# A finished attention pair leaves the accumulator bank later in the slot: ScalarE's part behind exponentials and copies, VectorE's part one slot on

## The chip, the cores and the metric

The kernel runs on one core of a Trainium2 chip. The metric is the device time of one execution, in microseconds. A core has TensorE (PE, matmuls and transposes into eight accumulator banks called PSUM), ScalarE (ACT: exponentials, copies), VectorE (DVE: reductions, multiplications, subtractions), GpSimd (POOL) and SyncE (SP), which here only load data. Each runs its own list of instructions; they meet by semaphores.

## What is computed

Two transformer blocks of two layers each, one after the other, on 512 tokens of width 1024, in float32. Precision is kept by splitting: every operand x of the large products is held as a high part and a low part x - high, and a product is three matmul passes. The parts that matter here are four attention stages. Cut to their core:

```python
# stage "fox" (first block, layer 2): 2 pairs of memory heads (256 keys), then 6 pairs of causal heads
logits = q @ k.T * scale + cum_logf[q] - cum_logf[k]; p = softmax(causal(logits)); o = p @ v
# stage "sparse" (second block, layer 1): 4 pairs of heads over chosen keys
p = softmax(where(chosen, q @ k.T * scale, -inf)); o = p @ v
# stage "dif" (second block, layer 2): 8 heads of two softmaxes each
a = softmax(q0 @ k0.T) - lam * softmax(q1 @ k1.T); o = a @ v
o = rms_norm(o, subln_g) * (1 - lambda_init)          # per head, then the output projection
```

The first memory attention (first block, layer 1) is a fourth stage of the same kind, which accumulates in one bank.

## The kernel before

The attention stages are one class, `Mixed` (line 1393). A stage has pairs of heads (in dif, a pair is one head with its two softmaxes). A pair is cut into four units, one for each 128 queries; unit `qt` of a causal pair sees `(qt+1)*128` keys. The stage runs in slots, numbered from 0. In slot s the three engines do, each in the order given:

- TensorE (`tensor`): the logits of unit s (L1481, L1487), half of the slot's share of projection matmuls, called fill (L430), the transposes of the probabilities of unit s-1 (`turn`, L1495), the product with the values of unit s-2 (`value`, L1519), the rest of the fill. The logits of unit s go into a pair of banks that unit s-2 used, so they wait for ScalarE's copy of the transposed probabilities of unit s-2 (signal `turned_act`).
- ScalarE (`scalar`): the exponentials of unit s (L1589, two instructions and their row sums), each waiting for VectorE's maximum; the copy of the transposed probabilities of unit s-1 (L1570); then, for a projection tile that has come in, in dif four part copies for the rotation (L698, only in even slots), and the high part of a weight strip (L369 or L373).
- VectorE (`vector`): the maxima of unit s (L1637 or L1640), the taking of projection tiles (L626, or in dif L705, L707, L709, which wait for L698), the low part of a weight strip (L396 or L401), the scaling of the probabilities of unit s (`scale`, L1616 to L1624), which waits for the exponentials.

In the sparse stage and from unit 24 of fox on (`t >= self.deep`) a third set of banks is used, the transposes lie one slot later, the copies of ScalarE stand ahead of the exponentials, and the scaling of unit s-1 stands ahead in VectorE's slot s.

The output of a pair (128 x 512) gathers in one bank. `self.outs` names it for each pair; in fox, sparse and dif two banks take turns. When a pair's fourth unit is done, `take_scalar` and `take_vector` empty the bank, in the slot that `taken_at` gives: slot 4n+6 for pair n, one later in the deep part. In fox and sparse ScalarE copies the bank out as the high part (L1672) and VectorE subtracts it from the bank for the low part (L1680). In dif ScalarE copies it to `difQ` (L1746) and squares that into `difK` (L1748); VectorE has nothing in `take_vector`. There the class `HeadNorm` goes on: in slot 26, at its end, TensorE sums the squares of heads 0 to 5 (`mean`, L1091), waiting for each; later slots take the root, spread it (L1098), scale each head (L1776), and form its high (L1756) and low part (L1781). In slots 26 to 31 some matmuls without a use (L1104) keep TensorE's clock up.

Before the change both takes stand early in their slot: ScalarE's is its first instruction, ahead of the copies and exponentials; VectorE's stands after the maxima and ahead of projection tiles and weight strips. A value product of pair n+2 waits for the emptying of pair n, four slots on.

Of the kernel before, what the change touches and what calls it, by code (L numbers as in the profile page):

```python
# [19 lines left out]
QT = SEQ // P  # L20
# [35 lines left out]
def build(nc, a, out):  # L56
    ctx = ExitStack()
    with ctx:
# [168 lines left out]
        class Signal:  # L227
# [3 lines left out]
            def __init__(self, name, engine):  # L231
                self.sem = ctx.enter_context(nc.semaphore(name))
                self.count = START
                self.engine = engine
                Signal.made.append(self)
# [60 lines left out]
        class NoErrands:  # L296
# [4 lines left out]
            def scalar(self, act, st):  # L301
                pass
# [1090 lines left out]
        class Mixed(Stage):  # L1393
# [6 lines left out]
            def __init__(self, pairs, sets, fill=(), pace=None, values_ready=None, apart=False, source=(hH, hL), norm=None, beside=None, probs=tmpB, turns=probsT,  # L1400
                         busy=(), busy_bank=0, deep=None, deep_sets=None, outs=None, first_use=(), last_split=None, late=None):
                super().__init__()
                self.busy, self.busy_bank = dict(busy), busy_bank
                self.pairs, self.sets, self.fill, self.apart, self.source = pairs, sets, fill, apart, source
                self.values_ready, self.norm, self.beside, self.probs, self.turns = values_ready, norm, beside, probs, turns
                self.units = [(n, pair, qt) for n, pair in enumerate(pairs) for qt in range(QT)]
                n = len(self.units)
                self.deep, self.outs, self.first_use = n if deep is None else deep, outs or [OUT_BANK] * len(pairs), dict(first_use)
                self.banks = [(sets if t < self.deep else deep_sets)[t % len(sets if t < self.deep else deep_sets)] for t in range(n)]
                self.buffers = list(sets) + [b for b in deep_sets or () if b not in sets]  # L1410
                lags = [1 if t >= self.deep else 0 for t in range(n)]
                self.slots = n + 3 + lags[-1]
                self.scaled_at, self.turned_at, self.valued_at, self.taken_at = [[[t for t in range(n) if t + later + lags[t] == s]
                                                                                  for s in range(self.slots + 2)] for later in (0, 1, 2, 3)]
                self.logits0, self.max0, self.exp0 = logits_in.reserve(2 * n), max_in.reserve(2 * n), exp_in.reserve(2 * n)
                self.scaled0, self.turned0, self.tact0 = scaled.reserve(n), turned_in.reserve(2 * n), turned_act.reserve(2 * n)
                self.value0 = value_in.reserve(n)
                self.gate = PairGate(pairs) if norm is None else norm.attach(pairs)
                self.taken0 = heads_taken.reserve(len(pairs)) if norm else 0
                self.before = [(bank_read[b], bank_read[b].count) for first in sets for b in (first, first + 1) if b < RING]  # L1420
                self.last_split, self.last_fill = last_split, fill[-1].strips[-1].tiles[-1] if fill else None
                self.late = late
                self.plan(pace)

            def plan(self, pace):
# [147 lines left out]
            def scalar(self, act):  # L1573
                units = len(self.units)
                for s in range(self.slots + 1):
                    for t in self.taken_at[s]:
                        if self.units[t][2] == QT - 1:
                            self.take_scalar(act, self.units[t][0])
                    for t in self.turned_at[s]:
                        if t >= self.deep:  # L1580
                            self.copy_turned(act, t)
                    if s < units:
                        n, pair, qt = self.units[s]
                        seen, bank = self.seen(s), self.bank(s)
                        for hh in range(2):
                            c = self.mine(s) + hh
                            act.wait_ge(max_in.sem, self.max0 + 2 * s + hh + 1)
                            to = self.prob(s, hh)[:, 0:seen]
                            act.activation(to, ps[:, bank + hh, 0:seen] if pair.row is None else to, ACT.Exp, bias=neg_max[:, c:c + 1],  # L1589
                                           scale=1.0 if pair.row is None else -1.0, accum_out=row_sum[:, c:c + 1]).then_inc(exp_in.sem, 1)  # L1590
                    for t in self.turned_at[s]:
                        if t < self.deep:
                            self.copy_turned(act, t)
                    for tile in self.copies[s]:
                        tile.strip.run.take.scalar_tile(act, tile)
                        if tile is tile.strip.tiles[-1] and (tile is not self.last_fill or self.last_split is None):
                            split_high(act, tile.strip.n + 2)
                    if self.last_split and s == self.last_split[0]:
                        split_high(act, self.last_fill.strip.n + 2)
                    if self.norm:  # L1600
                        self.norm.scalar_slot(act, s)
                    if self.late:
                        self.late.scalar_slot(act, s)
                    if self.beside:
                        self.beside.scalar_slot(act, s)
                if self.beside:
                    self.beside.scalar_rest(act)
# [18 lines left out]
            def vector(self, dve):  # L1626
                units = len(self.units)
                for s in range(self.slots + 1):
                    if s < units:
                        n, pair, qt = self.units[s]  # L1630
# [11 lines left out]
                    for t in self.scaled_at[s]:  # L1642
                        if t >= self.deep:
                            self.scale(dve, t)
                    for t in self.taken_at[s]:
                        if self.units[t][2] == QT - 1:
                            self.take_vector(dve, self.units[t][0])
                    if self.beside:
                        self.beside.vector_between(dve, s)
                    for tile in self.takes[s]:  # L1650
# [6 lines left out]
                    for t in self.scaled_at[s]:  # L1657
                        if t < self.deep:
                            self.scale(dve, t)
                    if self.norm:  # L1660
                        self.norm.vector_slot(dve, s)
                    if self.late:
# [1338 lines left out]
        for name, v in vectors:  # L3001
            r0, n = row_of[name], v.shape[0]
            while n:
# [3 lines left out]
                r0, n = r0 + m, n - m  # L3007
# [119 lines left out]
```

## Time and profile before

| | us |
|---|---|
| median of 3 runs | 2564.92 (2561.49 to 2565.49) |
| profiled execution, device time | 2560.56 |
| its span, first to last instruction | 2558.9 |
| TensorE busy | 2500.8 (98%) |
| VectorE busy | 1532.8 (60%) |
| ScalarE busy | 1053.4 (41%) |
| mean granted TensorE clock | 0.999 |

The span is what the trace shows; 1.7 us of the device time lie around it. A row of the timeline gives the start from the beginning of the span, the duration, the engine, the line of the kernel, the operation, output and inputs, and in brackets the idle time of the engine ahead of it with what ended it. Neighbouring equal instructions are merged (x4). A busy TensorE is not one at its peak, and ends of matmuls are modelled.

### The profile page before, as it was taken

The numbers are of one execution on the slowest core, as the hardware profiler recorded it, in microseconds if no ns is written. First come the engines' busy times: TensorE is split into PE (matmuls) and PEld (weight loads), VectorE is DVE, ScalarE is ACT, GpSimd is POOL, SyncE is SP. The second block draws the span as 40 slices with busy tenths as digits, with TensorE's granted clock in tenths as the row PEclk, the third lists the DMA queues.
The fourth block names the chain that finished last, engine by engine and source line by source line (L and its number), as shares of the span: only waits on it lengthen the run. The fifth ranks groups of instructions, "written<-read, shape, count | busy, mean of one in ns | idle before, by whom it ended". The sixth has DMA issues, their size and how long they took to land.

```text
span 2558.9 us, 31124 instructions
## 1 busy us (share of the span) xinstructions
PE 2500.8 (98%) x12413; PEld 1966.4 (77%) x12413; DVE 1532.8 (60%) x2299; ACT 1053.4 (41%) x1629; POOL 76.2 (3%) x154
## 2 busy tenths in 40 slices
PE   8999999999998999999999999999999989999999
PEld 6667877778866877777777578888878767888887
DVE  6996788686555487867667653333264775533334
ACT  5354433334555342323644743222254763522223
POOL 2000000000000001000000000000000000000000
PEclk9999999999999999999999999999999999999999
DMA  6123466553222256554321023323223112233321
GB/s 177 52 80 99 120 194 182 162 169 96 82 77 80 70 163 204 165 166 141 86 92 54 1 66 116 98 83 99 82 66 99 50 34 84 83 98 99 95 79 58
DMA packets 328095, 262.46 MB, mean 103 GB/s; under 512 B 13658, under 2 KB 312862, under 8 KB 327952
## 3 DMA queue, kind: packets, MB, share of 16 engines
q1 hardware_dynamic: 312256, 206.13, 27.2%
q0 software_dynamic: 15696, 54.34, 6.7%
q8 instruction: 99, 1.62, 0.3%
q14 instruction: 44, 0.36, 0.0%
HBM read 258.32 MB, written 2.12 MB: 102 GB/s over the span
## 4 chain that ended last, share of the span: by engine, by line
PE 88%; DVE 4%; ACT 4%; DVEq 1%; issue 1%; SPq 0%; DMA 0%; ACTq 0%; PEldq 0%; PEld 0%
PE ps L430 59%; PE ps L444 6%; PE ps L448 6%; PE ps L452 6%; PE ps L1481 2%; PE ps L2103 1%; PE ps L2631 1%; PE ps L1495 1%; PE ps L1519 1%; ACT tmpB L1589 1%; DVE wL L396 1%; ACT probsT L1570 1%; ACT wH L369 1%; ACT tmpA L698 1%; DVE tmpB L1640 0%
## 5 line engine op out<-in xcount | busy, mean ns | idle before, releaser
L396 DVE TENSOR_TENSOR wL<-raw,wH 128x2048 fp32r<-128x2048 f32 (+1 forms) x184 | 413.0, 2245 | 122.1 <-ACT wH L369 116.3
L369 ACT ACTIVATE wH<-raw 128x2048 fp32r<-128x2048 f32 (+1 forms) x184 | 343.7, 1869 | 237.1 <-PE ps L430 100.0
L430 PE MATMUL ps<-hH,wH 128*128 128x512 f32 x1656 | 427.7, 400 | 0.1
L430 PE MATMUL ps<-hH,wL 128*128 128x512 f32 x1656 | 425.2, 399 | 0.0
L430 PE MATMUL ps<-hL,wH 128*128 128x512 f32 x1656 | 424.8, 399 | 0.0
L430 PEld LDWEIGHTS ps<-hH,wH 128*128 128x128 f32 x1656 | 308.2, 188 | 84.7 <-issue 13.7
L430 PEld LDWEIGHTS ps<-hH,wL 128*128 128x128 f32 x1656 | 309.6, 188 | 82.4 <-issue 10.8
L430 PEld LDWEIGHTS ps<-hL,wH 128*128 128x128 f32 x1656 | 309.9, 188 | 76.4 <-issue 4.5
L1066 DVE TENSOR_TENSOR tmpB<-ps,tmpB 128x512 f32<-128x512 f32 x44 | 30.4, 691 | 228.2 <-PE ps L430 228.2
L1003 ACT ACTIVATE tmpA<-ff_up,cols 128x512 f32<-128x512 f32 x88 | 67.0, 809 | 237.9 <-DVEq L1030 237.9
L444 PE MATMUL ps<-gH,wH 128*128 128x512 f32 x480 | 154.6, 399 | 2.5 <-issue 1.0
L448 PE MATMUL ps<-gH,wL 128*128 128x512 f32 x480 | 153.1, 396 | 0.2 <-DVE wL L396 0.2
L452 PE MATMUL ps<-gL,wH 128*128 128x512 f32 x480 | 138.1, 396 | 0.0
L1040 DVE SCALAR_TENSOR_TENSOR tmpA<-ff_up,cols,tmpA 128x510 f32<-128x510 f32 (+1 forms) x176 | 124.3, 748 | 22.8 <-ACT tmpA L1003 17.1
L1964 DVE SCALAR_TENSOR_TENSOR mod_acc<-mod_ring,silu_c,mod_acc 128x1024 f32<-128x1024 f32 x84 | 107.7, 1282 | 45.6 <-DMA mod_ring<-w_mod 43.1
L1057 ACT ACTIVATE gH<-tmpB 128x512 fp32r<-128x512 f32 x44 | 27.8, 632 | 235.0 <-DVE tmpB L1066 235.0
L430 PE MATMUL ps<-gH,wH 128*128 128x512 f32 x480 | 122.8, 396 | 0.5 <-ACT mod L1993 0.5
L430 PE MATMUL ps<-gL,wH 128*128 128x512 f32 x480 | 122.4, 395 | 0.0
L430 PE MATMUL ps<-gH,wL 128*128 128x512 f32 x480 | 122.4, 395 | 0.0
L790 DVE SCALAR_TENSOR_TENSOR xT<-ps,mod_plus,xT 128x512 f32<-128x512 f32 x56 | 41.2, 748 | 133.8 <-PE ps L452 73.0
L444 PEld LDWEIGHTS ps<-gH,wH 128*128 128x128 f32 x480 | 90.2, 189 | 26.2 <-issue 2.9
L448 PEld LDWEIGHTS ps<-gH,wL 128*128 128x128 f32 x480 | 90.2, 188 | 22.3 <-DVE wL L396 1.0
(407 smaller groups left out, 3284.4 us busy)
## 6 DMA issues: line engine op xcount, KB each, us to landing
raw<-w_up SPq DMA_DIRECT2D x132, 512.0 KB, 5.3
mod_ring<-w_mod POOLq DMA_DIRECT2D x96, 512.0 KB, 4.3
raw<-w_down SPq DMA_DIRECT2D x32, 1024.0 KB, 5.9
raw<-w_gate SPq DMA_DIRECT2D x44, 512.0 KB, 4.0
raw<-w_down SPq DMA_DIRECT2D x16, 768.0 KB, 4.3
raw<-w_in_even SPq DMA_DIRECT2D x9, 1024.0 KB, 5.2
raw<-w_out SPq DMA_DIRECT2D x8, 1024.0 KB, 5.1
raw<-w_in_odd SPq DMA_DIRECT2D x16, 512.0 KB, 5.1
```

The source lines that it names most:

```text
L369: last = act.activation(wH[:, st.part, 0:st.size], raw[:, st.slot, 0:st.size], ACT.Copy)
L396: last = dve.tensor_tensor(wL[:, st.part, 0:st.size], raw[:, st.slot, 0:st.size], wH[:, st.part, 0:st.size].bitcast(F32), ALU.subtract)
L430: last = pe.matmul(dst, left, right, start=(t == 0 and k == 0), stop=(t == 2 and k == self.kt - 1))
L444: pe.matmul(dst, *operands(wH, srcH, k), start=(k == order[0]), stop=False)
L448: return pe.matmul(dst, *operands(wL, srcH, k), start=False, stop=False)
L452: return pe.matmul(dst, *operands(wH, srcL, k), start=False, stop=(k == order[-1]))
L790: dve.scalar_tensor_tensor(x, t, mod_plus[:, g:g + 1], x, ALU.mult, ALU.add).then_inc(bank_read[tile.bank].sem, 1)
L1003: last = act.activation(tmpA[:, 2 * u + f, :], ff_up[:, 2 * u + f, :], ACT.Identity, bias=self.bias(s, f), scale=self.weight(2, s, f))
L1040: dve.scalar_tensor_tensor(t, ff_up[:, 2 * u + f, 0:SEQ - back], self.weight(2 - back, s, f), t, ALU.mult, ALU.add)
L1066: dve.tensor_tensor(ff_tmp[:, s % 2, :], ps[:, value.bank, :], tmpB[:, s % 2, :], ALU.mult).then_inc(ff_prod.sem, 1)
L1481: mm = pe.matmul(ps[:, bank + hh, 0:seen], pair.q[lo:lo + DH, qt * P:qt * P + P], pair.k[lo:lo + DH, 0:seen], start=True, stop=True)
L1964: dve.scalar_tensor_tensor(mod_acc[:, :], mod_ring[:, u, :], silu_c[:, k:k + 1], mod_acc[:, :], ALU.mult, ALU.add).then_inc(mod_free[u], 1)
```

## The change

In stages whose output banks alternate (fox, sparse and dif; not the first memory attention), ScalarE's take moves from the head of the slot to behind the exponentials of unit s and the copy of unit s-1, still ahead of projection tiles and weight strips. VectorE's take moves to the end of the next slot's list, behind that slot's maxima, tiles, strips and scaling. No instruction is added or removed.

```diff
+                self.alternating = len(set(self.outs)) > 1
...
             def scalar(self, act):
                 for s in range(self.slots + 1):
-                    for t in self.taken_at[s]:
-                        if self.units[t][2] == QT - 1:
-                            self.take_scalar(act, self.units[t][0])
+                    done = [self.units[t][0] for t in self.taken_at[s] if self.units[t][2] == QT - 1]
+                    if not self.alternating:
+                        for n in done:
+                            self.take_scalar(act, n)
                     for t in self.turned_at[s]:
                         if t >= self.deep:
                             self.copy_turned(act, t)
...
                     for t in self.turned_at[s]:
                         if t < self.deep:
                             self.copy_turned(act, t)
+                    if self.alternating:
+                        for n in done:
+                            self.take_scalar(act, n)
                     for tile in self.copies[s]:
...
             def vector(self, dve):
-                    for t in self.taken_at[s]:
-                        if self.units[t][2] == QT - 1:
-                            self.take_vector(dve, self.units[t][0])
+                    if not self.alternating:
+                        for t in self.taken_at[s]:
+                            if self.units[t][2] == QT - 1:
+                                self.take_vector(dve, self.units[t][0])
...
                     for t in self.scaled_at[s]:
                         if t < self.deep:
                             self.scale(dve, t)
+                    if self.alternating and s:
+                        for t in self.taken_at[s - 1]:
+                            if self.units[t][2] == QT - 1:
+                                self.take_vector(dve, self.units[t][0])
```

## Rows read from the trace of the kernel before

**Rows 1.** The page, part 1: busy time, share of the span, instructions.
```profile
PE 2500.8 (98%) x12413; PEld 1966.4 (77%) x12413; DVE 1532.8 (60%) x2299; ACT 1053.4 (41%) x1629; POOL 76.2 (3%) x154
```

**Rows 2.** Busy time by stretch, fox and dif: PE, PEld, DVE, ACT, POOL; clock, DMA share, GB/s.
```profile
686.00:826.00 140.00, 128.06 (x871) 88.53 (x870) 80.76 (x258) 79.62 (x207) 8.18 (x15) 1.00 0.22 71
...
1964.00:2122.00 158.00, 145.02 (x843) 106.49 (x845) 110.26 (x292) 106.88 (x240) 5.05 (x9) 1.00 0.14 41
```

**Rows 3.** Groups by line: busy us, mean ns of one, idle before it.
```profile
L1672 ACT ACTIVATE gH<-ps 128x512 fp32r<-128x512 f32 x14 | 8.3, 589 | 3.0 <-PE ps L1519 3.0
L1680 DVE TENSOR_TENSOR gL<-ps,gH 128x512 fp32r<-128x512 f32 x14 | 9.5, 682 | 9.2 <-ACT gH L1672 9.2
L1746 ACT ACTIVATE difQ<-ps 128x512 f32<-128x512 f32 x8 | 4.7, 592 | 0.0
L1748 ACT ACTIVATE difK<-difQ 128x512 f32<-128x512 f32 x8 | 5.0, 631 | 0.6
```

**Rows 4.** Timeline, fox, slots 10 and 11.
```profile
730.59 0.58 ACT L1672 ACTIVATE gH<-ps 128x512 fp32r<-128x512 f32 x1
...
732.90 1.13 PE L1481 MATMUL ps<-foxK,foxQ 64*128 64x512 f32 x4 [1.49 <-ACT probsT L1570]
```

**Rows 5.** Timeline, fox, slots 14 to 16.
```profile
752.91 3.25 DVE L401 SCALAR_TENSOR_TENSOR wL<-raw,cols,wH 128x256 fp32r<-128x256 f32 x8
...
759.97 0.49 PE L1481 MATMUL ps<-foxK,foxQ 64*128 64x128 f32 x4 [0.98 <-ACT probsT L1570]
```

**Rows 6.** Timeline, fox, slot 27.
```profile
807.85 0.87 PE L1495 MATMUL ps<-ident,tmpB 128*128 128x128 f32 x6 [0.72 <-DVE tmpB L1624]
```

**Rows 7.** Timeline, fox, the last transposes.
```profile
819.55 0.66 PE L1495 MATMUL ps<-ident,tmpB 128*128 128x128 f32 x4 [0.17 <-DVE tmpB L1624]
```

**Rows 8.** Timeline, dif, slots 10 to 12.
```profile
2010.29 0.60 ACT L1746 ACTIVATE difQ<-ps 128x512 f32<-128x512 f32 x1
...
2013.81 0.62 ACT L1589 ACTIVATE tmpB<-tmpB,small 128x384 f32<-128x384 f32 x1 [2.22 <-DVE small L1640]
...
2015.42 2.39 ACT L698 ACTIVATE tmpA<-ps 32x512 f32<-32x512 f32 x4
...
2017.83 0.72 ACT L1589 ACTIVATE tmpB<-tmpB,small 128x512 f32<-128x512 f32 x1
...
2019.17 0.19 ACT L1589 ACTIVATION_READ_ACCUMULATOR tmpB<-tmpB,small 128x1 f32 x1
...
2019.46 0.49 ACT L1570 ACTIVATE probsT<-ps 128x384 f32<-128x384 f32 x1
...
2020.00 0.49 PE L1481 MATMUL ps<-difK,difQ 64*128 64x128 f32 x4 [0.21 <-ACT probsT L1570]
```

**Rows 9.** Timeline, dif, slots 23 and 24.
```profile
2075.10 0.69 DVE L705 SCALAR_TENSOR_TENSOR difQ<-ps,cosT 128x512 f32<-128x512 f32 x1
...
2078.74 0.44 PE L1495 MATMUL ps<-ident,tmpB 128*128 128x128 f32 x2 [1.36 <-DVE tmpB L1621]
```

**Rows 10.** Timeline, dif, slot 26.
```profile
2086.57 1.52 PE L1091 MATMUL ps<-difK,pick_mean 128*32 128x128 f32 x48
...
2087.65 0.36 ACT L1570 ACTIVATE probsT<-ps 128x256 f32<-128x256 f32 x1
```

**Rows 11.** Timeline, dif, slots 30 and 31.
```profile
2103.01 0.63 ACT L1748 ACTIVATE difK<-difQ 128x512 f32<-128x512 f32 x1
...
2103.54 0.60 ACT L1589 ACTIVATE tmpB<-tmpB,small 128x384 f32<-128x384 f32 x1
...
2105.15 1.13 PE L1481 MATMUL ps<-difK,difQ 64*128 64x512 f32 x4 [0.67 <-ACT probsT L1570]
...
2111.41 0.66 PE L1495 MATMUL ps<-ident,tmpB 128*128 128x128 f32 x4 [1.03 <-DVE tmpB L1621]
```

**Rows 12.** Busy time by stretch, first memory attention: TensorE's clock below one.
```profile
190.00:194.00 4.00, 4.00 (x31) 2.62 (x30) 2.79 (x4) 3.13 (x7) 0.00 (x0) 0.57 0.23 57
```

**Rows 13.** Timeline, first memory attention, just ahead of that.
```profile
188.82 0.66 PE L1495 MATMUL ps<-ident,mem_probs 128*128 128x128 f32 x4 [1.38 <-DVE mem_probs L1624]
```

## The prediction

> **What bounds the kernel now.** I read the page's busy shares first: TensorE is busy 98% of the span, VectorE 60%, ScalarE 41% [rows 1]. So a change on ScalarE and VectorE counts only where TensorE waits for them. The table by stretch then gives the room: TensorE is busy 128.1 of 140 us in fox and 145.0 of 158 us in dif [rows 2]. By the groups by line the moved work is small: 0.59 us on ScalarE and 0.68 us on VectorE for a pair of fox or sparse, 0.59 and 0.63 us, both on ScalarE, for a head of dif [rows 3]. Nothing is added, so the question is what each moved piece stood in front of, and what it stands in front of now. I followed that slot by slot in the timeline: at each of the 20 takes (8 in fox, 4 in sparse, 8 in dif) who waits, and which wait of TensorE comes next. Slots are numbered as in the code.
>
> **Fox, ScalarE's part.** Only in slot 10 does the copy stand in a row of work without idle time that ends in a wait of TensorE: copy at 730.59, exponentials, copy of the turned probabilities, and the logits of unit 11, which waited 1.49 us for it [rows 4]. The maximum was there already. Moved behind, the take costs nothing, since ScalarE then idles. Gain: from 730.59 to the next start at about 731.07, 0.48 us (0.58 less the 0.1 us by which neighbours overlap). In the other slots of the body ScalarE either waits for the maximum after the take, or TensorE arrives later by itself: 0.
>
> **Fox, VectorE's part.** In slot 14 the low part stood ahead of the weight strip that began at 752.91; behind that came scaling, the maximum of unit 15, its exponentials, the copy, and the logits of unit 16, which waited 0.98 us [rows 5]. The whole chain moves up by VectorE's step less overlap, 0.6 us, and the wait is longer than that, so all of it is gained. The subtraction now follows the scaling in slot 15, where VectorE next waits for those same logits: covered. In slots 6, 18 and 22 the maximum also comes earlier, but the next transposes follow projections or logits without a wait: 0. In slot 26 the low part stood ahead of the maximum and scaling whose end released the transposes at 807.85, which had waited 0.72 us [rows 6]; the maximum can move up only until the logits are there, so 0.5 us. In slot 31 the last transposes waited 0.17 us for scaling that followed the low part [rows 7]: 0.17. Sparse has the same pattern at its end; its other takes stand behind the scaling that TensorE waits for. I take 0.15 by rows 7. The last pairs of each stage have nothing behind them that could be passed. Sum of the gains: 0.48 + 0.6 + 0.5 + 0.17 + 0.15 = 1.9 us; between 1.1 (slots 10 and 14 alone) and 2.1.
>
> **Dif, slots 6, 10, 14, 18, 22.** Here the take goes the wrong way. It began at 2010.29 in idle time: ScalarE then waited 2.22 us for VectorE's maximum, which a weight strip holds up [rows 8]. So taking it away in front of the exponentials gives nothing. Its new place is behind the copy of unit 9 and ahead of the rotation's four copies, which began at 2015.42 and ran to 2017.81; the exponentials of unit 11 follow at 2017.83, their last row sum ends at 2019.36, the copy of unit 10 starts at 2019.46, and the logits of unit 12 had waited 0.21 us for that [rows 8]. ScalarE is full from 2013.81 to there, but for 0.1 us. The two steps add 0.59 + 0.63 = 1.22 us [rows 3]; off go this 0.1 and another 0.1, since a ScalarE instruction without a wait starts 0.1 before its predecessor's recorded end (2103.64 and 2103.54 in [rows 11]). So 1.0 us late for each head. The same order stands in all five slots, since a projection tile comes in every second slot and all five are even. TensorE doesn't catch up: rotations, strip and later exponentials hang on its own fill, so all shift together. For slot 22 I take 0.9: the next bound is the transposes at 2078.74, which wait for VectorE, and VectorE's rotation at 2075.10 can't start before the four copies end, at 2074.7 + 1.2 = 2075.9 [rows 9]. Sum: 4 x 1.0 + 0.9 = 4.9 us. Bounds for each: 0.8 if more overlaps, 1.3 if no slack is there: 4.0 to 6.5. Of VectorE nothing is moved here.
>
> **Dif, slot 26.** At the end of the slot TensorE sums the squares of heads 0 to 5, 48 matmuls in 1.52 us from 2086.57 [rows 10]; head 5 is the one whose square is made in this slot. Its eight come at about 2086.57 + 5/6 x 1.52 = 2087.8. The square will now be made behind the copy that ends at 2088.01 [rows 10], so it ends at 2088.0 - 0.1 + 1.3 = 2089.2. TensorE stands for 1.4 us, and behind it are the logits of unit 27, then maxima, exponentials, copy, logits of unit 28, a chain with idle time on both other engines. So +1.4 (1.2 to 1.6).
>
> **Dif, slot 30.** Here the take did stand in the way: the square ran to 2103.64, then the exponentials, the copy, and the logits of unit 31, which had waited 0.67 us [rows 11]. The maximum was in by 2102.5, so ScalarE gains 1.0. The logits gain at most their 0.67, but scaling and the maxima of VectorE gain nearly all, and the transposes at 2111.41 had waited 1.03 us for that chain [rows 11]: -1.0 (-0.7 to -1.0). In slot 34 no exponentials or copy are left, so the order stays: 0.
>
> **The sum.** Dif 4.9 + 1.4 - 1.0 = +5.3, fox and sparse -1.9: +3.4 us. On the profiled execution's 2560.6 us (span 2558.9) that is 2564.0. This execution lies 4.4 us under the median of the runs, 2564.9, and 1 us under their lowest. Counted from the median: 2568.3. Bounds of the sum: 4.0 + 1.2 - 1.0 - 2.1 = 2.1 and 6.5 + 1.6 - 0.7 - 1.1 = 6.3 us, 2567.0 to 2571.2.
>
> **The rivals.** *The late take is free.* With two banks nobody needs the full one for four slots, and ScalarE is busy only 106.9 of 158 us in dif [rows 2]; if its idle time took up the two steps, only the gains are left: 2564.9 - 1.9 - 1.0 = 2562.0. Against it: from 2013.81 to 2019.46 the rows show no such idle time, and the squares are needed in slot 26. The Trainium skill (Perfetto Trace Analysis, Optimizing Tensor Performance, Matmuls) advises rotating matmul groups through banks so that emptying one overlaps the next group. By that rule alone the dif term would be nil, which is this rival; the timeline agrees that no value product waits for a bank, but shows ScalarE's queue as what counts.
>
> *The clock falls,* the slower case. It would happen in slots 24 to 27 of dif, where waits of TensorE of 1.36 [rows 9] and the new 1.4 us lie close to each other without projections between. In the first memory attention a wait of 1.38 us [rows 13] came just before a stretch with a mean granted clock of 0.57 [rows 12], that is 3.4 of 4 us at 1.2 GHz. That costs at most half, 1.7 us: 3.4 + 1.7 = 5.1, 2570.0, or 2571.7 if it happens twice. It decides from the point at which the granted clock of those slots goes below 1. Against it: the matmuls without a use stand in just these slots, and waits of about this size in fox left the clock at 1.00 [rows 2]. The Trainium skill (TensorE: Matmul & The Clock Gate, Part 1) says that the clock is throttled by default and activity releases it; by it a longer stall speaks for this rival.
>
> *The gains in fox don't come,* as the subtraction, one slot later, holds the next maximum by its 0.6 us wherever VectorE isn't idle there: +5.3, 2570.2.
>
> That the order on the chip isn't the one written is not likely; it would give 2564.9.
>
> **How the numbers follow.** Forecast 0.67, free take 0.12, clock 0.10, no gain in fox 0.07, no effect 0.04. This kernel's measurement can tell about 0.2%, 5.1 us, from no change; the three runs alone are 4 us apart. Slower by more than that: half of the clock case and of the case without gains in fox with their upper bounds (0.09), and of the forecast the part above 5.1 us with the spread of the median (0.21): 0.30. Faster by more than 0.2%: half of the free take by that spread: 0.07. Within: 0.63. The range goes from the free take, 2562.0, to the upper bound with a fallen clock and the spread of runs, 2573.
>
> **What would show it.** Right: in dif the logits of units 8, 12, 16, 20 wait about 1.2 us for the copy, not 0.21; L1746 follows L1570 and precedes L698; L1091 has an idle time of about 1.4 us within it; the logits of unit 31 wait next to nothing; in fox those of unit 11 wait 1.0, those of unit 16 0.4. Dif grows from 158 by some 5 us, fox shrinks by some 1.7. Wrong: an unchanged 0.21 in dif (free take), a clock below 1 around slot 26, or waits of VectorE's maxima in fox that were not there.

## The result and the profile after

The changed kernel takes 2568.8 us (median of 18 runs, 2565.2 to 2571.0), the kernel before 2563.8 us in the same comparison (18 runs, 2561.5 to 2568.0). The ratio is 1.0019 with a 95% interval of 1.0013 to 1.0026: 5.0 us slower (3.3 to 6.7), where 3.4 us were forecast. That is inside the 0.2% that the prediction called no change, at its edge, and the whole interval lies on the slower side of one. The profiled execution took 2567.9 us, with a span of 2566.3 us.

The page's busy times of after answer to [rows 1].

```profile
PE 2505.5 (98%) x12413; PEld 1967.5 (77%) x12413; DVE 1533.8 (60%) x2299; ACT 1053.8 (41%) x1629; POOL 76.5 (3%) x154
```

The instructions are the same in number, and ScalarE and VectorE are as busy as they were to within 1 us. TensorE has 4.7 us more busy time for the same 12413 matmuls, which is the first sign that its clock was not the same. The table by stretch, fox and dif, answers to [rows 2] (columns as there).

```profile
686.00:825.50 139.50, 129.30 (x870) 89.37 (x869) 81.08 (x259) 80.26 (x208) 8.20 (x15) 0.99 0.22 70
1964.00:2128.00 164.00, 146.76 (x836) 107.73 (x835) 110.81 (x292) 106.95 (x240) 5.06 (x9) 0.98 0.13 40
```

Fox is 0.5 us shorter and dif 6 us longer, and the granted clock stands at 0.99 and 0.98 where both had 1.00. To split these lengths I took the start of each of TensorE's instructions in both traces and followed how the difference between the same instruction's two starts changes. A step in that difference is time lost or won at that place. Ahead of fox the difference already lies between -1.5 and +2.3 us in the twelve pairs of traces (0.5 for this one), which has nothing to do with the change; only steps count from here on.

In fox, first slots 10 and 11 and then the logits of unit 16, in the timeline of after (start, duration, engine, line, operation, idle time before and who ended it), beside [rows 4] and [rows 5].

```profile
732.26 0.58 ACT L1571 ACTIVATE probsT<-ps 128x512 f32<-128x512 f32 x1
732.74 0.58 ACT L1682 ACTIVATE gH<-ps 128x512 fp32r<-128x512 f32 x1
732.89 1.13 PE L1482 MATMUL ps<-foxK,foxQ 64*128 64x512 f32 x4 [1.00 <-ACT probsT L1571]
...
759.34 0.49 PE L1482 MATMUL ps<-foxK,foxQ 64*128 64x128 f32 x4 [0.39 <-ACT probsT L1571]
```

The high part (L1682) now stands behind the copy (L1571), and the waits are 1.00 and 0.39 us instead of 1.49 and 0.98: steps of -0.5 and -0.6. At the end of fox (slots 26 and 27, and the last transposes) the gain is smaller than forecast.

```profile
805.93 0.69 DVE L1645 CUSTOM_DVE_ANT_0 tmpA<-ps,gate_rows 128x512 f32<-128x512 f32 x1 [0.23 <-PE ps L1488]
...
808.20 0.87 PE L1496 MATMUL ps<-ident,tmpB 128*128 128x128 f32 x6 [0.50 <-DVE tmpB L1629]
...
819.66 1.09 PE L1496 MATMUL ps<-ident,tmpB 128*128 128x128 f32 x8
```

VectorE's maximum can move up only until its logits are there, and now it waits 0.23 us for them; so the wait of the transposes goes from 0.72 [rows 6] to 0.50 only. The last transposes wait no more (0.17 before, [rows 7]).

In dif, slots 10 to 12, the stretch of [rows 8]:

```profile
2016.14 0.36 ACT L1571 ACTIVATE probsT<-ps 128x256 f32<-128x256 f32 x1
...
2016.41 0.58 ACT L1756 ACTIVATE difQ<-ps 128x512 f32<-128x512 f32 x1
...
2017.07 0.63 ACT L1758 ACTIVATE difK<-difQ 128x512 f32<-128x512 f32 x1
...
2017.72 2.40 ACT L698 ACTIVATE tmpA<-ps 32x512 f32<-32x512 f32 x4
...
2020.14 0.72 ACT L1591 ACTIVATE tmpB<-tmpB,small 128x512 f32<-128x512 f32 x1
...
2021.48 0.19 ACT L1591 ACTIVATION_READ_ACCUMULATOR tmpB<-tmpB,small 128x1 f32 x1
...
2021.69 0.49 ACT L1571 ACTIVATE probsT<-ps 128x384 f32<-128x384 f32 x1
...
2022.23 0.49 PE L1482 MATMUL ps<-difK,difQ 64*128 64x128 f32 x4 [1.33 <-ACT probsT L1571]
```

The two steps of the take lie between the copy and the rotation's four copies, ScalarE runs through, and the logits of unit 12 wait 1.33 us, not 0.21. The steps at units 8, 12, 16 and 20 are +1.11, +1.13, +1.12 and +1.12. At slot 24 it is +0.86: VectorE's rotation waits for ScalarE's fourth copy, and the transposes of [rows 9] wait for what VectorE does behind it.

```profile
2080.43 0.69 DVE L705 SCALAR_TENSOR_TENSOR difQ<-ps,cosT 128x512 f32<-128x512 f32 x1 [0.75 <-ACT tmpA L698]
...
2084.08 0.66 PE L1496 MATMUL ps<-ident,tmpB 128*128 128x128 f32 x4 [1.07 <-DVE tmpB L1626]
```

Then slots 26, 30 and 31, beside [rows 10] and [rows 11]:

```profile
2091.92 1.30 PE L1091 MATMUL ps<-difK,pick_mean 128*32 128x128 f32 x40
...
2094.60 0.43 PE L1091 MATMUL ps<-difK,pick_mean 128*32 128x128 f32 x8 [1.39 <-ACT difK L1758]
...
2111.35 1.13 PE L1482 MATMUL ps<-difK,difQ 64*128 64x512 f32 x4
...
2117.29 0.66 PE L1496 MATMUL ps<-ident,tmpB 128*128 128x128 f32 x4 [0.71 <-DVE tmpB L1626]
```

The 48 matmuls over the squares break after 40 and wait 1.39 us for head 5's. The logits of unit 31 don't wait now, and the transposes behind wait 0.71, not 1.03: steps of -0.74 and -0.33. The view of TensorE's waits in dif (waited for, us in total, times, longest) sums it up; first before, then after.

```profile
PE ps L1481 <- ACT probsT L1570: 5.3, 16, 1.1
```

```profile
PE ps L1482 <- ACT probsT L1571: 9.9, 14, 1.3
...
PE ps L1091 <- ACT difK L1758: 1.4, 1, 1.4
```

One item isn't in any wait. The output projection's first eight matmuls behind dif:

```profile
2125.72 1.95 PE L444 MATMUL ps<-gH,wH 128*128 128x512 f32 x4 [0.96 <-issue]
2127.45 1.91 PE L448 MATMUL ps<-gH,wL 128*128 128x512 f32 x4
```

Before, the first four took 1.2 us and the next 1.1:

```profile
2119.84 1.18 PE L444 MATMUL ps<-gH,wH 128*128 128x512 f32 x4 [0.96 <-issue]
```

The table by stretch shows why, there and at two other places of after's trace (the granted clock is the figure behind POOL's, as in [rows 2]):

```profile
797.00:802.00 5.00, 4.52 (x30) 3.12 (x32) 3.95 (x9) 3.44 (x6) 0.00 (x0) 0.66 0.34 100
...
2084.00:2089.00 5.00, 4.85 (x24) 3.78 (x25) 3.02 (x14) 4.64 (x13) 0.00 (x0) 0.66 0.01 2
...
2125.00:2130.00 5.00, 4.28 (x25) 2.93 (x26) 1.91 (x3) 2.26 (x3) 1.86 (x4) 0.66 0.10 26
```

A mean of 0.66 over 5 us is 3.4 us at 1.2 GHz and the rest at 2.4 GHz. The first such stretch took about 1.2 us from fox's gain, the last one about 1.5 us at the projection; the one at 2084.9 took next to nothing, as the waits of 0.27, 0.32 and 0.91 us that stand behind it in before's trace took it up. The profiled execution of before had a mean clock of 0.999, and its 27 executions beside the first experiments 0.9979 in the mean, so a typical execution of the kernel before has low stretches that its one trace doesn't show.

### The profile page after: what moved, and what is told of

Its sections match the earlier page's. It is cut to its first block, busy times and chain, and to the rows that moved or that the text cites. A ratio compares the mean times of both kernels' runs of the same rounds, so it can differ in the third digit from the quotient of the medians.

```text
span 2566.3 us, 31124 instructions
## 1 busy us (share of the span) xinstructions
PE 2505.5 (98%) x12413; PEld 1967.5 (77%) x12413; DVE 1533.8 (60%) x2299; ACT 1053.8 (41%) x1629; POOL 76.5 (3%) x154
## 4 chain that ended last, share of the span: by engine, by line
PE 87%; DVE 5%; ACT 4%; DVEq 1%; issue 1%; DMA 1%; ACTq 0%; SPq 0%; PEldq 0%; PEld 0%
PE ps L430 58%; PE ps L444 6%; PE ps L448 6%; PE ps L452 6%; PE ps L1482 2%; PE ps L2113 1%; PE ps L1520 1%; PE ps L2641 1%; PE ps L1496 1%; DVE wL L396 1%; ACT tmpB L1591 1%; DMA raw<-w_in_a 1%; DVE tmpB L1645 1%; ACT probsT L1571 1%; ACT tmpA L698 1%
## 5 line engine op out<-in xcount | busy, mean ns | idle before, releaser
L430 PEld LDWEIGHTS ps<-hH,wH 128*128 128x128 f32 x1656 | 307.8, 188 | 85.1 <-issue 13.7
```

The costliest lines, as they stand in the source:

```text
L430: last = pe.matmul(dst, left, right, start=(t == 0 and k == 0), stop=(t == 2 and k == self.kt - 1))
```

## The experiments

Eight heads or pairs are taken in dif and in fox. For the experiments the one flag of the change was made into two sets, of the numbers `n` whose take ScalarE makes late and of those whose low part VectorE makes late, so that each part can be had alone.

```diff
-                self.alternating = len(set(self.outs)) > 1
+                two = len(set(self.outs)) > 1
+                self.late_act = {n for n in range(len(pairs)) if two and (norm is None)}
+                self.late_dve = {n for n in range(len(pairs)) if two and (norm is None)}
...
-                    if not self.alternating:
-                        for n in done:
+                    for n in done:
+                        if n not in self.late_act:
                             self.take_scalar(act, n)
```

`norm is None` holds in fox and sparse, not in dif; VectorE has no part in dif's take. In each experiment below only the conditions inside the brackets differ; where `late_dve` isn't shown it is empty. The kernel before ran beside all of them. Times are medians, differences are to the kernel before of the same chip.

**Fox and sparse alone.**

```diff
+                self.late_act = {n for n in range(len(pairs)) if two and (norm is None)}
+                self.late_dve = {n for n in range(len(pairs)) if two and (norm is None)}
```

> Only fox and sparse change; dif is as before. Theory A (each take counts by what stands behind it in its slot): TensorE is ahead of the kernel before by 0.5 us from slot 11 of fox, by 1.1 us from slot 16, by 1.3 at slot 27, by 1.5 at the end of fox and 1.6 at the end of sparse, and the end comes 1.6 us earlier (ratio 0.9994). Theory B (the loss of the change is mostly stretches at 1.2 GHz that the moved takes cause): fox has such a stretch here in every execution, as the changed kernel's profile has at 798 us, and the gain is nil or less.

Measured: 2560.9 against 2563.1 us, ratio 0.9994 (0.9985 to 1.0003). The trace has the steps of the changed kernel: -0.48 at unit 11, -0.61 at unit 16, then, by the end of fox, +0.73, because a stretch at 1.2 GHz stands in this trace too:

```profile
797.00:802.00 5.00, 4.96 (x38) 3.86 (x40) 3.95 (x9) 3.28 (x7) 0.00 (x0) 0.66 0.32 86
```

In sparse the step is -0.19. The interval includes one, so the time alone doesn't show the gain; the steps do. Two traces of later experiments without such a stretch show what slot 27 and the last transposes are worth together: -0.49 in both.

**Dif alone.**

```diff
+                self.late_act = {n for n in range(len(pairs)) if two and (norm is not None)}
+                self.late_dve = {n for n in range(len(pairs)) if two and (False)}
```

> Only dif changes; fox and sparse are as before. Theory A: TensorE loses 1.1 us at each of the logits of units 8, 12, 16 and 20, 0.9 at the transposes of slot 24, 1.4 within the squares of slot 26, and wins 1.0 in slots 30 and 31: +5.7 us before the output projection, ratio 1.0022. Theory B: less than 3 us from waits, the rest from stretches at 1.2 GHz; the mean granted clock is below that of the kernel before in every execution.

Measured: 2569.5 against 2563.1 us, ratio 1.0027 (1.0018 to 1.0036). The steps are +1.15, +1.13, +1.11, +1.13, +0.85, +1.60, -0.74 and -0.33, in sum +5.9. So the loss is dif's alone, and the two stages don't act on each other.

**Head 5 alone** (its square is the one made in slot 26).

```diff
+                self.late_act = {n for n in range(len(pairs)) if two and (norm is not None and n == 5)}
```

> Only head 5 of dif (slot 26) moved. Theory A: TensorE stands for 1.4 us within the 48 matmuls of the squares and all after it is 1.4 us later; nothing else of the stage moves. Free take: no idle time there.

The trace has one step of more than 0.1 us in dif, at this stall:

```profile
2089.50 0.43 PE L1091 MATMUL ps<-difK,pick_mean 128*32 128x128 f32 x8 [1.39 <-ACT difK L1758]
```

The whole group then ran from 2086.82 to the next at 2089.86, 3.04 us, where it had taken from 2086.57 to 2088.02, 1.45 us: a step of 1.6, that is the wait of 1.39 and 0.2 more for breaking a row of matmuls that ran without a gap. The single time is 2563.1 us, as before, and can't show 1.6 us.

**Heads 0 to 4 alone.**

```diff
+                self.late_act = {n for n in range(len(pairs)) if two and (norm is not None and n < 5)}
```

> Only heads 0 to 4 of dif (slots 6, 10, 14, 18, 22) moved. Theory A: four steps of 1.1 us at the logits of units 8, 12, 16, 20 and one of 0.9 at slot 24, nothing at slots 26 and 30: +5.3 us at the end of the stage. Free take: 0.

Steps +1.19, +1.13, +1.12, +1.12 and +0.84, in sum +5.4, and about 1.5 more from a stretch at 1.2 GHz at the start of the projection; one time of 2569.4 against 2563.9 us. The five heads are nearly the whole of dif's loss, and the clock can fall at the projection without the stall of slot 26.

**Heads 0 to 4, the square made twice.** If the price of a late take is ScalarE's time for it and nothing else, one more step of the same kind must show in full.

```diff
                 act.drain()
+                if n < 5:
+                    act.activation(difK[:, n, :], difQ[:, n, :], ACT.Square)
+                    act.drain()
                 act.activation(difK[:, n, :], difQ[:, n, :], ACT.Square).then_inc(squares.sem, 1)
```

> As the run with heads 0 to 4 moved, but each of these squares is made twice, with a drain between (the same values are written again). Theory A, ScalarE is full from the take to the logits: the second square (0.63 us and 0.08 of drain) comes on top in full, each step is 1.8 us instead of 1.1. If ScalarE had idle time behind the take, the step would grow by less than half of 0.7.

```profile
2016.61 0.63 ACT L1759 ACTIVATE difK<-difQ 128x512 f32<-128x512 f32 x1
2017.31 0.63 ACT L1761 ACTIVATE difK<-difQ 128x512 f32<-128x512 f32 x1
...
2022.46 0.49 PE L1484 MATMUL ps<-difK,difQ 64*128 64x128 f32 x4 [2.02 <-ACT probsT L1573]
```

The second square starts 0.70 us after the first, and the logits wait 2.02 us, 0.69 more than 1.33. The steps are 1.77, 1.82, 1.81 and 1.8, slot 24 +1.54, so ScalarE's time is passed on one to one. This trace also has 3.4 us at 1.2 GHz in the middle of dif, at 2044.9, 1.7 us behind a wait of 2.04 us, which cost 1.6 us, and 6.8 us at 2126.8. The time is 2572.4 us, 3.0 over the one without, but these two single executions differ by as much ahead of dif and by the clock, so it says little; the steps carry the reading.

**Heads 0 to 4, one place later:** the take behind the rotation's four copies, ahead of the next exponentials.

```diff
-                    if self.alternating:
-                        for n in done:
-                            self.take_scalar(act, n)
                     for tile in self.copies[s]:
                         tile.strip.run.take.scalar_tile(act, tile)
...
+                    for n in done:
+                        if n in self.late_act:
+                            self.take_scalar(act, n)
```

> Heads 0 to 4 moved still further, behind the rotation's four copies and ahead of the next slot's exponentials. Theory A in its simple form (what counts is that the take stands ahead of the exponentials of unit s+1, which are released early): the same steps of 1.1 us. Rival: the rotation on VectorE, which waits for the four copies, is what holds the chain; then the steps shrink, since the copies are no longer late. At slot 24, where VectorE's rotation is the bound by the prediction, the step should change: with the copies on time the bound is the scaling behind the late exponentials, about 0.5 us instead of 0.9.

```profile
2014.90 2.39 ACT L698 ACTIVATE tmpA<-ps 32x512 f32<-32x512 f32 x4
2017.32 0.60 ACT L1756 ACTIVATE difQ<-ps 128x512 f32<-128x512 f32 x1
2018.00 0.63 ACT L1758 ACTIVATE difK<-difQ 128x512 f32<-128x512 f32 x1
2018.54 0.70 ACT L1593 ACTIVATE tmpB<-tmpB,small 128x512 f32<-128x512 f32 x1
...
2019.85 0.18 ACT L1593 ACTIVATION_READ_ACCUMULATOR tmpB<-tmpB,small 128x1 f32 x1
2019.94 0.47 ACT L1573 ACTIVATE probsT<-ps 128x384 f32<-128x384 f32 x1
...
2020.46 0.49 PE L1484 MATMUL ps<-difK,difQ 64*128 64x128 f32 x4 [1.19 <-ACT probsT L1573]
```

The steps are 0.97, 0.98, 0.99 and 0.99: the price hardly depends on the place, as long as the place lies in the row of work that runs without idle time. Of the 0.14 us that are left off, some 0.1 stand where the copy starts: 0.09 ahead of the row sum's recorded end here (2019.94 against 2020.03), 0.02 behind it in the changed kernel. The square overlaps the exponentials behind it (2018.63 against 2018.54) by as much as the take overlapped the copy in the changed kernel. At slot 24 it is +0.42, not +0.85, as VectorE's rotation no longer waits for copies held up by the take. The time was 2566.0 against 2563.9 us, with a stretch of 6.8 us at 1.2 GHz at 2120.6 in it, which cost about 2.5 us.

**Fox and sparse, ScalarE's part alone.** The high part late, the low part where it was.

```diff
+                self.late_act = {n for n in range(len(pairs)) if two and (norm is None)}
+                self.late_dve = {n for n in range(len(pairs)) if two and (False)}
```

> Fox and sparse with ScalarE's take late and VectorE's early, as before; dif as before. Theory A: VectorE's low part waits for the high part, so it now waits for ScalarE behind exponentials and copies. In slot 10 the logits of unit 11 still gain 0.5 us, but VectorE's strip stands behind the later low part; in slots 14, 26 and 31 no gain, and a loss where VectorE's waiting lands on the path: at the logits of unit 16, as the high part is now made only behind the copy that ends at 754.4, some 2 us later than the low part stood before. Rival (the gain is ScalarE's alone): 0.5 us at slot 11 and nothing lost.

This is the most expensive kernel of the study: 2575.5 against 2563.9 us. Slots 14 to 16:

```profile
756.67 0.59 ACT L1682 ACTIVATE gH<-ps 128x512 fp32r<-128x512 f32 x1
...
757.30 0.69 DVE L1690 TENSOR_TENSOR gL<-ps,gH 128x512 fp32r<-128x512 f32 x1 [2.56 <-ACT gH L1682]
...
757.91 3.25 DVE L401 SCALAR_TENSOR_TENSOR wL<-raw,cols,wH 128x256 fp32r<-128x256 f32 x8
...
762.11 0.87 PE L1498 MATMUL ps<-ident,tmpB 128*128 128x128 f32 x6 [2.01 <-DVE tmpB L1631]
...
762.70 0.72 ACT L1593 ACTIVATE tmpB<-tmpB,small 128x512 f32<-128x512 f32 x1 [5.43 <-DVE small L1647]
```

VectorE stands idle for 2.56 us in front of the subtraction, with the weight strip of 3.25 us queued behind it, then the scaling for which the transposes wait 2.01 us, then the maxima for which ScalarE waits 5.43 us. The steps add up to +13.7 us in fox, with four stretches at 1.2 GHz in them, the third of 6.8 us, and +2.4 in sparse. The gain at unit 11, -0.47, is there. How much of the sum is the clock's was not taken apart; the wait alone at the transposes of slot 16 is a step of 2.2.

**Fox and sparse, VectorE's part alone.**

```diff
+                self.late_act = {n for n in range(len(pairs)) if two and (False)}
+                self.late_dve = {n for n in range(len(pairs)) if two and (norm is None)}
```

> Fox and sparse with ScalarE's take early, as before, and VectorE's one slot late; dif as before. Theory A: the high part is there early, so nothing waits; the 0.5 us of slot 11 are missing, the 0.6 at unit 16, 0.2 to 0.4 at slot 27 and 0.2 at the end stay: 1.0 to 1.2 us ahead at the end of fox, without stretches at 1.2 GHz. Rival (what matters is ScalarE's place): no gain.

```profile
734.75 1.13 PE L1484 MATMUL ps<-foxK,foxQ 64*128 64x512 f32 x4 [1.48 <-ACT probsT L1573]
...
761.20 0.49 PE L1484 MATMUL ps<-foxK,foxQ 64*128 64x128 f32 x4 [0.39 <-ACT probsT L1573]
...
809.61 0.88 PE L1498 MATMUL ps<-ident,tmpB 128*128 128x128 f32 x6 [0.52 <-DVE tmpB L1631]
```

Unit 11 waits its old 1.48 us; unit 16, slot 27, the last transposes and sparse have their gains. So of fox's gains only unit 11's is ScalarE's, and the rest is VectorE's. No stretch at 1.2 GHz was expected; there is one in fox, at 794.8, which took 0.7 us, and 6.8 us at 2119.2, which took 2.6. The single time of 2564.6 us (2561.7 before) therefore says nothing against the gains.

**Only what pays:** fox and sparse late, and in dif head 6, whose take stood in the way in slot 30.

```diff
+                self.late_act = {n for n in range(len(pairs)) if two and (norm is None or n == 6)}
+                self.late_dve = {n for n in range(len(pairs)) if two and (norm is None)}
```

> Fox and sparse as changed, in dif only head 6 (slot 30) moved. Theory A: -1.6 us from fox and sparse, -1.0 us from slots 30 and 31 of dif: 2.6 us faster than before, ratio 0.9990. Free take: like the changed kernel without any loss, and the changed kernel would not be slower than this one.

Measured: 2560.2 against 2563.1 us, ratio 0.9991 (0.9982 to 1.0000). Steps -0.6, -0.63, -0.49, -0.20 in fox and sparse, -0.66 and -0.32 at slots 30 and 31:

```profile
2110.93 0.66 PE L1498 MATMUL ps<-ident,tmpB 128*128 128x128 f32 x4 [0.71 <-DVE tmpB L1628]
...
2117.00:2125.00 8.00, 6.78 (x34) 4.99 (x35) 2.76 (x5) 3.94 (x6) 3.49 (x7) 0.57 0.27 84
```

The second line, of the table by stretch, is this trace's low stretch at the projection, 6.8 us long; it took 2.6 us from that execution.

**The waits filled.** To take the clock out of the comparison, 16 matmuls without a use were put into waits of dif's end: 4 in slot 24 ahead of the transposes, 3 at the head of slot 26, 3 each in slots 33 and 34, and 3 behind the last. The changed kernel's new wait of 1.39 us at the squares was not filled. It was done once with only what pays late and once with the changed kernel's order; the last two lines of the edit are one argument of a longer line.

```diff
+                    if self.norm and s == 26:
+                        keep_busy(pe, 0, 3)
...
+                    if self.norm and s == 24:
+                        pe.wait_ge(self.norm.free[0][0].sem, self.norm.free[0][1])
+                        keep_busy(pe, 0, 4)
...
+                if self.norm:
+                    keep_busy(pe, self.busy_bank, 3)
...
-busy={**{s: (3, 2) for s in range(26, 32)}, 32: (0, 8)}
+busy={**{s: (3, 2) for s in range(26, 32)}, 32: (0, 8), 33: (0, 3), 34: (0, 3)}
```

> The kernel with the kept gains (fox and sparse as changed, of dif head 6 alone), with 3 or 4 more matmuls without a use in the waits of TensorE in dif: slots 24, 26, 33, 34 and at the end of the stage. Theory B' (stretches at 1.2 GHz around the end of dif cost about 1 us per execution in the mean): the mean clock over the executions rises from 0.9971 to that of the kernel before (0.9979) or above and the time falls by about 1 us, to 3.5 us under before (ratio 0.9986). Rival: the fillings cost as much as they save, or the stretches lie elsewhere: ratio 0.9991 as without them.

> The changed kernel with the same fillings. Theory B': of its 5 us, 4 to 4.5 come from waits and the rest from the clock; with the fillings 1 us comes back, ratio 1.0016, and no stretch at 1.2 GHz stands at slot 24 or at the start of the output projection of dif. Rival: 1.0019 as without them, with the clock stretches still there.

Measured: 2558.8 us with what pays, ratio 0.9990 (0.9982 to 0.9999), and 2566.0 us with the changed order, ratio 1.0016 (1.0006 to 1.0025), against 2561.7 us. The first is 2.8 us under the kernel before, which is what it gained without the filling too: the 1 us more that was expected (ratio 0.9986) did not come. The changed order came out at the expected 1.0016, but its interval also holds the rival's 1.0019. Neither trace has a low stretch in dif or at the projection; of the changed order, filled:

```profile
2084.00:2089.00 5.00, 4.15 (x31) 3.05 (x29) 3.50 (x12) 4.06 (x10) 0.00 (x0) 1.00 0.01 2
...
2125.00:2130.00 5.00, 5.00 (x36) 3.70 (x35) 1.65 (x2) 1.64 (x2) 1.22 (x3) 1.00 0.05 13
```

The steps of the changed order are the same as without the filling: +1.16, +1.13, +1.13 and +1.12 for the first four, and behind the first added matmuls +0.83 at slot 24, +1.60, -0.74 and -0.33. So the filling cost nothing. Outside dif both traces do have low stretches. The changed order has one of 3.4 us at 792.8 in fox, and what pays one of 6.8 us at 1288.1:

```profile
1288.00:1295.00 7.00, 7.00 (x14) 4.03 (x14) 3.72 (x5) 2.92 (x4) 0.00 (x0) 0.51 0.15 53
```

This one cost 3.2 us, and TensorE had waited no longer than 0.3 us in the 30 us ahead of it.

**All timed kernels side by side.** The first column is the sum of the steps as the traces without low stretches give them (fox -1.6, sparse -0.2, slots 30 and 31 -1.1, the rest of dif +7.0), so without the clock.

| kernel | sum of steps | measured difference | mean granted clock, and before's beside it |
|---|---|---|---|
| changed | +4.1 us | +5.0 us | 0.9965, none for before |
| dif alone | +5.9 | +6.4 | 0.9965, 0.9979 |
| fox and sparse alone | -1.8 | -2.2 | 0.9971, 0.9979 |
| only what pays | -2.9 | -2.8 | 0.9971, 0.9979 |
| only what pays, filled | -2.9 | -2.8 | 0.9980, 0.9981 |
| changed, filled | +4.1 | +4.3 | 0.9979, 0.9981 |

The sums lie within 1 us of every measurement, and each interval is some 2 us wide to either side. The clock is averaged over all executions of a kernel (11 or 18, of before 27 and 21), each read to 0.001.

## Why the prediction was right, and where its terms were off

The forecast was 2568.3 us and the time is 2568.8. That the two lie within 0.5 us is partly luck: the forecast counted from a median of three runs that was 1.1 us above the median of 18, and its sum was 1.6 us below the measured difference. The sum was +3.4; the steps of the traces give +4.1, and the measured difference is 5.0 with an interval (3.3 to 6.7) that holds both. By the steps' own numbers:

- **Where the take stands in dif.** The order in five slots, the row of work without idle time, and the shift of everything behind it together are as read from [rows 8]. Doubling the square (+0.69 for each) and moving the take behind the rotation (still +0.98) show that the price is ScalarE's own time for it in that row and not the place or the bank.
- **The size of it was a tenth short.** Forecast 1.0 for each of four, measured 1.12. The step said 1.22 less 0.1 of idle time less 0.1 of overlap. The idle time did go (the last row sum ends at 2021.67, the copy starts at 2021.69). The overlap of 0.1 is there, between the copy that ends at 2016.50 and the take that starts at 2016.41, but the square waits for the copy it reads, and that leaves a gap of 0.08 between 2016.99 and 2017.07. Overlap and gap cancel, and 4 x 0.12 = 0.5 of the 0.7 us by which the sum was short come from that.
- **Slot 24:** forecast 0.9, measured 0.86, by the bound that was named: VectorE's rotation now waits 0.75 us for the fourth copy. Behind the rotation instead, the step is 0.42, so it was this bound.
- **Slot 26:** the wait was forecast at 1.4 and is 1.39. The step is 1.6, the upper end of the bounds, since TensorE also pays 0.2 us for the break itself, which the step had not counted. Units of dif that already waited 0.21 us pay nothing of the kind: there the step equals the difference of the waits.
- **Slots 30 and 31:** forecast -1.0, measured -1.07, part of it at the logits and the rest at the transposes, as said.
- **Fox:** -0.48 and -0.6 forecast for units 11 and 16, -0.5 and -0.6 measured, and the run with VectorE's part alone shows each engine's share as stated. Slot 27 is the term that failed: the step took 0.5 with the reason that the maximum can move up only until the logits are there, but how far that is was not read from the trace. It is about 0.2: the wait went from 0.72 to 0.50 and the step is 0.21 to 0.25. The last transposes' step is 0.24 (forecast 0.17), sparse's 0.19 (forecast 0.15).

Of the rivals, *the late take is free* is refuted by the run with dif alone, +6.4 us. The Trainium skill's rule behind it (Perfetto Trace Analysis, Optimizing Tensor Performance, Matmuls), that groups of matmuls should rotate through banks so that emptying one overlaps the next group, holds for the bank itself: no trace shows a matmul waiting for it. It says nothing of what stands behind the emptying instruction on its own engine, and that is what cost here. *No gains in fox* is refuted by the trace with fox and sparse alone, whose steps are all there; its time alone (0.9985 to 1.0003) couldn't do it.

*The clock falls* was given one chance in ten, for slots 24 to 27 alone. A clock below 1 around slot 26 was also one of the prediction's signs of being wrong, and it came (0.66 from 2084 to 2089), though nearly without a price. It came from another place than the rival said: the stretch begins at 2084.9, behind the waits of 1.33 and 1.07 us of slot 24 and ahead of the stall of 1.39 us, and none of the four traces that have this stall (the changed kernel, dif alone, head 5 alone, changed and filled) has a low stretch in the 30 us behind it. The clock also falls at two places that the prediction did not name: in fox, where by before's trace it had taken waits of this size as harmless, and at the start of the output projection, where it costs about 1.5 us of the profiled execution (the rival's bound was 1.7). At the end of dif and the start of the projection five of the six unfilled traces with a late take among dif's first six heads have a low stretch (all but head 5 alone), but so have two of the four experiments that leave these heads untouched (only what pays, and VectorE's part alone); before's trace and the two filled ones have none. Over all executions the mean clock of the changed kernel is 0.9965 and that of the filled one 0.9979. Within one kernel's runs an execution is about 1 us longer for each 0.001 that its mean clock is lower (1.1 for before, 27 runs; between 0.6 and 1.7 in the other sets but one, fox and sparse alone, which has it the other way). By that some 1.4 us of the changed kernel's time would be the clock's. But the measured difference between unfilled and filled is 0.7 us, less than their intervals, and with only what pays late it is nil. So the lower clock of the changed kernel is shown, and that it is back with the filling; what it is worth in the median is not shown, only that the sums of the steps leave less than 1 us for it. The prediction looked for the fall only in slots 24 to 27; the stretches at the projection began beside the waits at the stage's end (1.10, 1.00 and 0.96 us), which are old.

Open is why the clock falls between 793 and 802 us in the traces of kernels with fox changed (the changed kernel, fox and sparse alone, each engine's part alone, changed and filled), but not in the two with only what pays late, whose fox is the same, nor in any with fox as it was. The wait of 1.61 us ahead of it is the same in all 13 traces, before's too, and the next is 1.56 us in all but three: with ScalarE's part alone it is 1.36, and in two the clock had already fallen between the two waits. Filling these waits was not tried.

## What to carry to other kernels

Before an instruction is moved, read what runs behind it at its new place without idle time up to the next wait of the engine that bounds the kernel: if there is such a row, the move costs its full duration there, however idle the engine is on average, and the same move can pay in one slot and cost in the next. Idle time in front of an instruction that waits for another engine (here ScalarE's 2.2 us ahead of the exponentials) is a free place, so a take that stood there was well placed; choose the place slot by slot rather than by one flag for all. Don't move a producer later and leave its consumer early on another engine: ScalarE's half alone took 11.6 us more in its one timed execution, because VectorE waited with a weight strip queued behind, low stretches of the clock included. The consumer alone could move: VectorE's half alone kept its gains.

## What the runs showed of the hardware

In the 13 traces TensorE's clock fell from 2.4 to 1.2 GHz for 3.4 us, sometimes for 6.8, 26 times in the attention stages and at the start of the projection behind dif, and once elsewhere, at 1288.1 (the first 20 us and the end of the kernel aside). Each of the 26 stretches began during a wait of TensorE of 0.96 to 2.04 us or at most 1.7 us behind its end. The reverse doesn't hold: waits of 1.61 and 1.56 us in fox left the clock at 1.00 in before's trace and in others, and the stall of 1.39 us at the squares had no fall close behind it in any of its four traces. Nor is such a wait needed, as the stretch at 1288.1 shows. What one costs depends on what lies under it: 1.5 us where matmuls run without a gap (2125.8), next to nothing where waits take it up (2084.9), 2.6 to 3.2 us for a stretch of 6.8 us. The Trainium skill (TensorE: Matmul & The Clock Gate, Part 1) has the clock throttled by default and released by activity; the two filled traces agree in so far as they have no low stretch in dif, and none of the 16 added matmuls is visible in the steps. One trace of each can't show more.

A break in a row of matmuls costs more than the wait that the profile prints: 1.6 us between starts for a wait of 1.39 at 2089.50, as the matmuls around it no longer run into each other. The ends of matmuls are modelled, so the wait is the less certain of the two.
